# A streaming-encoder step on eight cores: an opening whose loads no longer wait for landings, W0 first on GpSimd's queue, and TensorE's planned pauses filled with matmuls on zeros

## The reference

```python
u = rmsnorm(x, norm_mix)
xl, gl, xp, gp, ml, mp = split(u @ w_in)          # 1024 -> 5632 columns
xc = causal_conv(xl)                              # width 4
r, i = sigmoid(xc @ w_rg_a + b), sigmoid(xc @ w_rg_i + b)   # block diagonal
a = exp(-8 * r * softplus(-lam)); h = scan(a, sqrt(1 - a*a) * i * xc)
lru_out = h * silu(gl)
pooled = trailing_mean(xp, windows 2/4/8/16) - xp
pool_out = (pooled @ w_pool + b_pool) * pool_scale * silu(gp)
x = x + (sigmoid(ml) * lru_out + sigmoid(mp) * pool_out) @ w_out
x = x + sigmoid(rmsnorm(x, norm_ple) @ w_ple_gate) * (p @ w_ple)
y = rmsnorm(x, final_norm)
```

## Time and profile before

| | us |
|---|---|
| median of 3 runs | 988.4 (987.76 to 992.04) |
| the profiled execution | 988.52 |
| its span, core 2, the slowest | 987.0 |
| spans of the eight cores | 978.2 to 987.0 |

### The profile page before, as it was taken

The page is one execution under the profiler, slowest core; times in us unless marked ns, Lnnn a source line. Parts: engine busy times, 40 slices in busy tenths (PEclk is TensorE's granted clock), DMA queues, the critical chain, the costliest instruction groups (busy, mean ns, idle before and its releaser), DMA issues.

```text
span 987.0 us, 17018 instructions; the slowest of 8 cores (978.2 to 987.0 us)
## 1 busy us (share of the span) xinstructions
PE 941.2 (95%) x4630; PEld 441.8 (45%) x4720; DVE 786.5 (80%) x1222; ACT 780.9 (79%) x1300; POOL 277.4 (28%) x558
## 2 busy tenths in 40 slices
...
GB/s 167 200 220 231 181 190 220 169 196 236 220 190 167 118 192 226 200 219 164 171 155 204 151 190 208 226 135 151 232 159 211 107 137 214 241 200 205 222 77 122
DMA packets 111071, 183.11 MB, mean 186 GB/s; under 512 B 65281, under 2 KB 69889, under 8 KB 110978
## 3 DMA queue, kind: packets, MB, share of 16 engines
...
q0 software_dynamic: 10224, 18.94, 13.4%
...
## 4 chain that ended last, share of the span: by engine, by line
PE 77%; ACT 7%; DMA 5%; issue 5%; DVE 4%; POOL 1%; SPq 0%; DVEq 0%; ACTq 0%; POOLq 0%
PE psum L922 52%; PE psum L1325 10%; PE psum L1291 8%; DMA xb<-xp 3%; PE psum L1332 2%; PE psum L1006 1%; PE psum L1009 1%; DMA ut<-ub 1%; PE psum L1172 1%; DMA ring<-win_bf 1%; DVE wk L986 1%; DMA wpg<-w_in 1%; ACT wk L1030 0%; DVE ub L867 0%; ACT L1176 0%
## 5 line engine op out<-in xcount | busy, mean ns | idle before, releaser
L922 PE MATMUL psum<-ut,ring 128*128 128x512 bf16 x2416 | 549.9, 379 | 8.9 <-ACT wk L1176 1.9
L922 PEld LDWEIGHTS psum<-ut,ring 128*128 128x128 bf16 x2464 | 239.7, 98 | 294.8 <-issue 9.0
L986 DVE SCALAR_TENSOR_TENSOR wk<-xw,cvec,wk 128x512 f32<-128x512 f32 x183 | 133.2, 745 | 28.9 <-ACT wk L974 21.5
L1325 PE MATMUL psum<-wpg,u2t 128*128 128x512 bf16 x502 | 117.8, 379 | 0.7
L1291 PE MATMUL psum<-wout,mg 128*128 128x512 bf16 x506 | 115.9, 379 | 0.7 <-ACT wk L974 0.3
L825 POOL TENSOR_SCALAR stat<-stat 128x1 f32<-128x1 f32 x98 | 41.1, 420 | 233.8 <-ACT wk L1345 86.5
L922 PE MATMUL psum<-ut,wpg 128*128 128x512 bf16 (+1 forms) x390 | 82.6, 364 | 1.9 <-ACT ut L878 1.2
L1325 PEld LDWEIGHTS psum<-wpg,u2t 128*128 128x128 bf16 x512 | 49.9, 98 | 60.2 <-issue 0.6
L1291 PEld LDWEIGHTS psum<-wout,mg 128*128 128x128 bf16 x512 | 49.8, 98 | 59.6 <-issue 1.3
L827 POOL TENSOR_TENSOR stat<-stat,negh 128x1 f32<-128x1 f32 x98 | 67.9, 694 | 9.5 <-POOL stat L825 0.2
L1071 POOL COPY hst<-wk 128x1 f32<-128x1 f32 x46 | 37.3, 817 | 104.2 <-DVE wk L1066 91.9
(11 more groups left out here) (201 smaller groups left out, 1518.8 us busy)
## 6 DMA issues: line engine op xcount, KB each, us to landing
ring<-win_bf SPq DMA_DIRECT2D x150, 512.0 KB, 4.6
...
wpg<-w_in POOLq DMA_DIRECT2D x11, 512.0 KB, 11.6
...
```

The costliest lines, as they stand in the source:

```text
L922: nd("pe", pe_cost(8, N // cuts), [lambda e, kc=kc, a=a, z=z: e.matmul(b.ap[:, a:z], lhsT=s.ap.rearrange("p (k n) -> p k n", k=8)[:, kc, o ...
L986: nd("dve", dve_cost(N), lambda e, j=j, w=w: e.scalar_tensor_tensor(out=av(), in0=xw()[:, :, 3 - j:W - j], scalar=w, in1=av(), op0=ALU.mul ...
L1325: nd("pe", pe_cost(8, 512), [lambda e, hf=hf, kc=kc, eb=eb, u2t=u2t: e.matmul(eb[hf].ap, lhsT=u2t.ap.rearrange("p (k n) -> p k n", k=8)[:, ...
```

## The change

1. **x loads.** The gates of x4 to x7 are gone; their due times follow x0 to x3. The norm vector is loaded straight into row 0 of `gmbc`, so that no xb buffer is taken for it. With six xb buffers, x0 to x5 can be issued at once, x6 and x7 when the first two buffers have been read. cvec's load stands behind x4's on SP's queue, no longer first.
2. **W loads.** `wg` is now -1, 0, 2, 4, 5, 6, 7: W0 has no gate and is GpSimd's first instruction; W1 is gated on x0's power, W2 on x2's, W3 on x4's, W4 on x5's, W5 on x6's. wa and wi, which stood right behind W2 on GpSimd's queue, now stand behind W5.
3. **Fillers.** Where the planner's own clock sees a pause of over 500 ns before a TensorE node that it starts before 45000 ns, it puts matmuls on zeros in front of that node: as many as fill the pause less 300 ns at 0.84 ns for each column. They write into the columns that the node will overwrite, 256 columns wide or, for the four-piece projection, 128. The zeros are 256 columns of `uts`, set by VectorE. There are 53 of them, 27 with 256 columns and 26 with 128.
4. **Planner.** `penw` is 1.548 for 2.764, `slack` 4.921 for 27.396, `pes` 49.979 for 20.158; every number of `ORDER` is new. So the order of all engines differs over the whole program, with the same instructions but for the fillers, their memset, and the choice of ScalarE or VectorE for two copies of transposes.

```diff
-           a2=0.944, an=0.2, cs=12784.442, wl=30305.046, pes=20.158, late=[0, 1, 2, 3], wq='sp', wd=6037.115, pet=2,
+           an=0.2, cs=12784.442, wl=30305.046, pes=49.979, late=[0, 1, 2, 3], wq='sp', wd=6037.115, pet=2,
...
-           xp=291.224, gp=607.324, ml=-525.777, mp=-632.501, tn=1289.017, dvn=-1050.698, tab=400.0, xg=(0, 0, 1, 1),
-           wg=[0, 2, 3, 4, 5, 6, 7], wbn=40452.849, nr=5, nu=3, nx=3, ac=3)
+           xp=291.224, gp=607.324, ml=-525.777, mp=-632.501, tn=1289.017, dvn=-1050.698, tab=400.0,
+           wg=[-1, 0, 2, 4, 5, 6, 7], wbn=40452.849, fl=45000.0, fm=300.0, nr=5, nu=3, nx=3, ac=3)
...
-ORDER = {"a0.0": 10635, "a0.1": 14621, "a0.2": 17428, "a0.3": 67864, "a1.0": 1423, "a1.1": 10731, "a1.2": 13857,
+ORDER = {"a0.0": -5265, "a0.1": -847, "a0.2": -2424, "a0.3": -3738, "a1.0": -288, "a1.1": -96, "a1.2": 1144,
...
+        if n.eng == "pe":
+            gap = n.start - self.pe_end
+            if n.start < PRM["fl"] and gap > 500.0:
+                a, z = n.cols
+                for k in range(int((gap - PRM["fm"]) // (0.84 * (z - a)))):
+                    n.ops.append(P.op("pe", lambda e: e.matmul(
+                        n.writes[0][0].ap[:, a:z], lhsT=self.fill.ap[:, 0:128], rhs=self.fill.ap[:, 0:z - a],
+                        start=True, stop=True), reads=[self.fill.slot.bufs[0]], writes=[wb[0]]))
+            self.pe_end = n.end
...
+    Z.fill = UTS
+    nd("dve", 150, lambda e: e.memset(UTS.ap[:, 0:256], 0.0), writes=[UTS], nom=-99500)
...
-       writes=xb2(row), nom=-98000, nbytes=30, queue="act")
+       writes=xb2(GM), nom=-98000, nbytes=30, queue="act")
...
     def first_x(dst, j):
-        gates = []
-        if j >= 4:
-            gates = [gate(PRM["xg"][j - 4])]
-        n = load(dst, x_src(tiles[j // 4], j % 4), -90000 + 2000 * j if j < 4 else -22000 + 1000 * j, 1650, gates=gates)
+        n = load(dst, x_src(tiles[j // 4], j % 4), -90000 + 2000 * j, 1650)
...
-                n = load(s, d_w_in[m], -25000.0 + 2000 * k if p == 0 and k < 4 else nom - PRM["wl"], 3100, queue="pool")
+                n = load(s, d_w_in[m], -89000.0 + 9000 * k if p == 0 and k < 6 else nom - PRM["wl"], 3100, queue="pool")
                 if p == 0:
                     w_first.append(n)
                     want = PRM["wg"][min(k, len(PRM["wg"]) - 1)]
-                    if want < len(pow_first):
+                    if want < 0:
+                        pass
+                    elif want < len(pow_first):
                         Z.after(n, pow_first[want])
...
-        load(CV, d_vecs, -83000, 200)
+        load(CV, d_vecs, -79500, 1500)
```

More of the change, by code:

```diff
@@ L17 @@
 NPAIR = IN_COLS // 256
[L18 to L19 removed]
+PRM = dict(window=76081.776, lim=113076.056, lag=10050.77, penw=1.548, slack=4.921, evac=0, p2=0, c2=0.552, a2=0.944,
+           an=0.2, cs=12784.442, wl=30305.046, pes=49.979, late=[0, 1, 2, 3], wq='sp', wd=6037.115, pet=2,
            a1=-14793.788, host=7, sc=0.5, slag=24170.975, hb=2, lb=2, ws=14, sl=2966.681, sy=1594.855, sw=2176.42,
            pg=13578.55, dl=500.0, inf=1.0, wa=6000.0, wp=55540.826, rf=2, rw=4, gm=1000.0, xl=-544.564, gl=-1280.812,
[L22 to L25 removed]
[62 rows of a table removed]
+           xp=291.224, gp=607.324, ml=-525.777, mp=-632.501, tn=1289.017, dvn=-1050.698, tab=400.0,
+           wg=[-1, 0, 2, 4, 5, 6, 7], wbn=40452.849, fl=45000.0, fm=300.0, nr=5, nu=3, nx=3, ac=3)
+ORDER = {"a0.0": -5265, "a0.1": -847, "a0.2": -2424, "a0.3": -3738, "a1.0": -288, "a1.1": -96, "a1.2": 1144,
[63 rows of a table added]
 class Buf:
@@ L290 @@
     __slots__ = ("eng", "cost", "fns", "reads", "writes", "nom", "tset", "npred", "succs", "ready", "end", "vs",
-                 "queue", "nbytes", "seq", "lane", "holds", "ops", "start", "port", "alt", "soft", "nb", "gates", "paced", "tag")
+                 "queue", "nbytes", "seq", "lane", "holds", "ops", "start", "port", "alt", "soft", "nb", "gates", "paced", "tag", "cols")
 LAT = {"pe": 270.0, "act": 220.0, "dve": 190.0, "pool": 260.0, "sp": 60.0}
@@ L307, in __init__ @@
         self.tag = ""
+        self.pe_end = 0.0
+        self.fill = None
     def pool(self, name, slots, reserve=0):
@@ L320, in node @@
     def node(self, eng, cost, fns, reads=(), writes=(), nom=0.0, tset=None, nbytes=0, queue=None, lane=None,
-             holds=(), alt=None, soft=0.0, nb=0.0, gates=(), paced=False):
+             holds=(), alt=None, soft=0.0, nb=0.0, gates=(), paced=False, cols=(0, 256)):
         n = Node()
         n.nb = nb
+        n.cols = cols
         n.gates = list(gates)
@@ L608, in build_program @@
     WPOOL = fix("wpool", [128, 4 * 256], BF16)
-    GM = fix("gmbc", [128, 1024], F32)
+    GM = fix("gmbc", [128, 1024], F32, nsub=2)
     G3 = fix("g3bc", [128, 1024], F32)
@@ L771, in build_program @@
     Z.tag = "cv"
-    ones, row = Z.val("ws"), Z.val("xb")
+    ones = Z.val("ws")
+    Z.fill = UTS
+    nd("dve", 150, lambda e: e.memset(UTS.ap[:, 0:256], 0.0), writes=[UTS], nom=-99500)
     nd("pool", 100, lambda e: e.memset(ones.ap[0:1, :], 32.0), writes=[ones], nom=-99000)
-    nd("act", 100, lambda e: e.dma_start(out=row.ap[0:1, :], in_=d_norm_mix.unsqueeze(0)),
-       writes=xb2(row), nom=-98000, nbytes=30, queue="act")
+    nd("act", 100, lambda e: e.dma_start(out=GM.ap[0:1, :], in_=d_norm_mix.unsqueeze(0)),
+       writes=xb2(GM), nom=-98000, nbytes=30, queue="act")
     for hf in range(2):
```

12 lines of the change are left out of this document (5 added, 7 removed), and 125 rows, old and new, of the table ORDER.

## The result

| | before | after |
|---|---|---|
| median of the runs, us | 988.3 (987.76 to 992.04) | 977.9 (975.85 to 980.67) |
| profiled execution, us | 988.52 | 975.85 |
| its slowest core, us | 987.0 | 974.3 |
| mean span of the eight cores, us | 983.7 | 971.4 |
| mean end of the fourth transposes of tile 1, us | 45.5 | 39.1 |

The ratio of the times is 0.989, 95% interval 0.985 to 0.993: faster by about 10 us. The profiled execution of the changed kernel was its quickest, so the two traces differ by 12.2 to 12.7 us where the medians differ by 10.4. All readings are of core 2 unless another is named.

The account below looks back on a forecast made before the run. TensorE, busy 941.2 of 987.0 us, was taken as the bound. From 988.4 us, 4.2 for the opening and 0.7 for passing on, with nothing for the rest, gave 983.5 us, range 974 to 993.

Parts of the forecast that it names:

- Size of the opening: Fourth transposes of tile 1 on core 2 end at 41.2 us instead of 45.4, a gain of 4.2 us.
- How the loads share: W0 shares the DMA engines with x0 to x3: x0 lands at 7.0 to 9.9 us, x3 13.9, x5 23.1.
- x5's square with two copies behind it at 23.1: On ScalarE, x5's square waits for its landing at 23.1 us, delaying tile 0's last two copies to 25.5.
- W0 with tile 0 done at 28.0: TensorE finishes W0's projections of tile 0 at 28.0 us, 4 us later than before.
- Clock, 1 us: TensorE's clock drops after the hole from about 21 to 25.5 us, adding 1 us (0 to 2).
- fillers, 0.4 us: All fillers on TensorE together cost 0 to 3.3 us, taken as 0.4.
- wi: Load of wi follows wa, now behind W5, so up to 3 us of wait at the gate matmuls is possible.
- Passing on: What the opening gains reaches the end fully, and a little more: 0.7 us on top of 4.2.
- I take the new as equal: TensorE's idle time after 50 us stays at 17 us, with 4 us either way.
- x5 lands early: Rival, 0.18: x5 lands at 20.3 or 17.4 us, fourth transposes at 36 to 38, gain 7 to 9: 980 us.
- The gain is eaten: Rival, 0.23: x5 at 27 us or later with the clock down, or late gate weights, leave no gain: 988 us.
- Slower: Rival, 0.15: the new order starves TensorE after the opening, doubling idle time from 17 to 34 us: 996 us.

Follow-up runs that it names:

- r7: Changed kernel with W0 issued behind x0's power, as in the kernel before, and x0 to x7 still without gates: 979.2 us, ratio to before 0.990.
- r5: Changed kernel with ScalarE's copies of tile 0's transposes moved ahead of the squares of x2 to x5: 978.3 us, ratio to before 0.990.
- r1: Changed kernel with its 53 fillers left out and everything else as it is: 977.9 us, ratio to before 0.992.
- the ten runs with the new order: Changed kernel (three runs) and seven variants with its order but other loads, fillers or copy places: 975.3 to 982.3 us.
- the four and the ten: Four kernels with the old order (before, and three with new x or W0 loads), 987.3 to 988.9 us; ten runs with the new order, 975.3 to 982.3.

## Why the prediction was right, and which step of it was wrong

The forecast was 983.5 (974 to 993); the median is 977.9. The range held it, and "faster" had the largest chance. The gain was forecast at 4.9 us and measured at 10.4; about half of it has the cause that was forecast. By its steps:

- **Size of the opening.** 41.2 forecast for core 2, 40.2 measured. The number is right, with wrong parts inside.
- **How the loads share.** x0 was to land at 7.0 to 9.9; its square starts at 4.5. No term stood for cvec, whose place ahead of x0 was worth 1.3 to 1.8 us (r7's reading above). x3 was to land at 13.9, and does so at 17.7. I had let W0 delay all four, with W1 moving only from 14; its issue is at 6.76, and it moved beside x2 and x3. The rule that I had weighed and put aside, from the Trainium skill, "DMA: Bandwidth & Descriptors", Queues, rings and completion order (queues with work are served in turn), fits these landings and the equal bytes of the two queues: each x that is behind a W comes one W later, and x5 is there by 22.46 although W2 was issued at 19.43. What I held against it, x4's landing at 26.8 in the old kernel, was no sharing at first: x4 and x5 were issued at 16.66, and from 16 to 20 us GpSimd's queue alone moved anything:

```profile
q0 software_dynamic: 181, 0.68, 102.7%
```

SP's queue moves its first 0.02 MB between 20 and 21 us. Why it began only 4 us after the issue is not settled.
- **x5's square with two copies behind it at 23.1.** It stands at 22.46, but waits for no landing. The hole is real (5.8 us of waits for ut), but most of it is at x2 and x3. And r5 shows that the copies' place in the queue was not the cause: the rows themselves were. "W0 with tile 0 done at 28.0": the last narrow group begins at 27.45. The right number came from two errors that cancel: a less crowded start and a more crowded middle.
- **Clock, 1 us; fillers, 0.4 us.** The four fillers in the path cost 0.43 (31.80 to 32.23), and r1 shows no cost of all 53: right. The 1 us for the clock was of the right size: the last two full groups at half pace (19.58, 22.98) take 0.8 each over full pace, partly inside waits. It was not tried apart.
- **wi.** The gate matmuls wait 1.10 us for it: "up to 3 us" was right.
- **Passing on.** Over the 80 core spans of the ten runs with the new order, the span changes by 1.04 us (standard error 0.12) for each us of T4. "Fully passed on" was right; the 0.7 us on top, 0.17 for each us of the 4.2, is neither shown nor excluded.
- **"I take the new as equal", 17 us idle after 50 us.** This is the step that failed. The order after the opening is worth 4.4 us of span (rest 937.4 to 933.0, means of the four and the ten) although it holds 0.9 us more work of TensorE, the four gate matmuls moved there: 5.3 us less of everything else, of which the waits after 50 us make up most (9.5 to 10.7 us with the old order, 5.1 to 6.6 with the new). I had written that a difference of more than 4 would prove me wrong; on core 2 it is 11.7 by the windows and 8.0 by the waits, and 5.6 by the waits as a mean over the cores. The term was taken as zero with 4 us either way; it measured about 5. With it the sum comes out: 6.4 less 0.9 for the opening, 5.3 for the rest, 10.8 us against the measured 10.4.
- **Rivals.** "x5 lands early" named 980, the nearest time, and its premise held (x5 before W2), but its consequence, T4 at 36 to 38, did not: core 2 is at 40.2. That its time came close is luck, for the missing part came from the order behind the opening. "The gain is eaten" has its wait for wi and no more. "Slower" fell: from 75 to 100 us TensorE loses 0.3 us instead of 3.2, with ScalarE still busy 24.82 of 25.

What the runs don't settle is which moves of the new order bring its 5 us. The waits after 50 us that went are known (xcb before gate matmuls 2.0 to 0.3 us, ScalarE's wk 5.2 to 2.9, ut by DMA 0.9 to nothing, ScalarE's xpw 1.0 to nothing, as means over the cores); which instruction's new place removed each was not tried. Nor was the new order run with the old places of W1 to W5, wa and wi, so their part in the 5 us is open too.
